# Two of four token tiles get their expert dots from TensorE for all experts, and gather the scores with the values in one row

## The reference, cut to what matters

```python
def peer(h, w_q, keys, u_tab, v_tab):        # u_tab, v_tab: 16384 experts x 1024
    tok = h.reshape(-1, 128, 1024)           # four tiles of 128 tokens
    def block(xb):
        q = (xb @ w_q).reshape(T, 8, 2, 128)
        s = jnp.einsum('thpd,hpnd->thpn', q, keys)
        sv, si = lax.top_k(s, 16)
        cand = sv[:, :, 0, :, None] + sv[:, :, 1, None, :]      # 16 x 16 per head
        cv, ci = lax.top_k(cand.reshape(T, 8, 256), 16)
        eid = i1 * 128 + i2                                     # 8 x 16 = 128 experts per token
        g = jax.nn.softmax(cv, axis=-1)
        u = jnp.take(u_tab, eid, axis=0)
        act = jax.nn.gelu(jnp.einsum('thkd,td->thk', u, xb))
        return jnp.einsum('thk,thkd->td', g * act, jnp.take(v_tab, eid, axis=0))
```

## Time and profile before

| | us |
|---|---|
| median of three runs | 2097.53 (2096.0 to 2109.05) |
| profiled execution: its span, from the first to the last instruction | 2089.7 |
| time around the span, if the profiled execution was as long as the median | 7.8 |
| first gather issued | 582.8 |
| last gather issued | 2067.2 |

### The profile page before, as it was taken

The page is one execution under the profiler, slowest core; times in us unless marked ns, Lnnn a source line. Parts: engine busy times, 40 slices in busy tenths (PEclk is TensorE's granted clock), DMA queues, the critical chain, the costliest instruction groups (busy, mean ns, idle before and its releaser), DMA issues.

```text
span 2089.7 us, 15934 instructions
## 1 busy us (share of the span) xinstructions
PE 1518.5 (73%) x4648; PEld 876.7 (42%) x4648; DVE 1491.0 (71%) x2906; ACT 497.1 (24%) x1412; POOL 878.6 (42%) x658
## 2 busy tenths in 40 slices
PE   7899999889667778887865778655555555556564
PEld 3465787668545555564531445311111111111111
DVE  2545368763276667878598856688898898898876
ACT  2201120111222233223233322222222223222222
POOL 2478404220033333343345434345554555455553
PEclk9899899999879899999987899877777767676677
DMA  8233221124278999999999999799999999999997
GB/s 348 101 139 138 89 79 61 62 77 144 81 308 353 362 351 345 410 392 387 421 393 361 386 378 347 282 413 387 413 412 422 403 409 387 409 417 409 406 418 294
DMA packets 90604, 647.28 MB, mean 310 GB/s; under 512 B 10413, under 2 KB 10773, under 8 KB 12565
## 3 DMA queue, kind: packets, MB, share of 16 engines
q0 software_dynamic: 76448, 555.78, 66.7%
q1 hardware_dynamic: 13376, 90.25, 11.2%
q10 hardware_dynamic: 693, 0.23, 0.0%
HBM read 644.12 MB, written 2.10 MB: 309 GB/s over the span
## 4 chain that ended last, share of the span: by engine, by line
PE 42%; DMA 21%; DVE 19%; issue 8%; ACT 7%; POOL 2%; SPq 0%; DVEq 0%; ACTq 0%; POOLq 0%
DMA arena<-in_peer_uv,arena 21%; PE bank L917 13%; PE bank L671 11%; DVE arena L1642 6%; PE bank L887 6%; PE bank L856 4%; DVE arena L1657 3%; PE bank L707 3%; POOL arena L613 2%; ACT smalls L1138 2%; ACT arena L1133 1%; ACT arena L1128 1%; PE bank L906 1%; PE bank L697 1%; PE bank L800 1%
## 5 line engine op out<-in xcount | busy, mean ns | idle before, releaser
L613 POOL DMA_INDIRECT arena<-in_peer_uv,arena x512 | 688.8, 1345 | 901.4 <-DVE arena L1657 571.1
L917 PE MATMUL bank<-arena,smalls 128*128 128x512 f32 x1024 | 700.9, 822 | 477.6 <-ACT smalls L1138 470.7
L1642 DVE CUSTOM_DVE_ANT_0 arena<-arena 128x1024 f32<-128x1024 f32 x512 | 615.1, 1221 | 87.5 <-DMA arena<-in_peer_uv,arena 86.1
L917 PEld LDWEIGHTS bank<-arena,smalls 128*128 128x128 f32 x1024 | 225.7, 241 | 887.8 <-ACT smalls L1138 675.2
L1657 DVE SCALAR_TENSOR_TENSOR arena<-arena 128x1024 f32<-128x1024 f32 x252 | 322.0, 1278 | 204.8 <-ACT arena L1133 204.8
L671 PE MATMUL bank<-arena 128*128 128x256 f32 (+1 forms) x1216 | 336.1, 433 | 3.6 <-ACT arena L962 3.4
L671 PEld LDWEIGHTS bank<-arena 128*128 128x128 f32 x1216 | 235.9, 195 | 104.6 <-issue 76.0
L1128 ACT ACTIVATE arena<-arena 128x2 f32<-128x2 f32 x256 | 51.9, 203 | 778.0 <-DVE arena L1642 776.3
L887 PE MATMUL bank<-arena 128*128 128x256 f32 x512 | 125.4, 402 | 0.7 <-issue 0.7
L1133 ACT ACTIVATE arena<-arena 128x1 f32<-128x1 f32 x512 | 122.9, 287 | 8.5
L887 PEld LDWEIGHTS bank<-arena 128*128 128x128 f32 x512 | 106.2, 208 | 35.9 <-issue 21.5
(11 more groups left out here) (241 smaller groups left out, 1311.5 us busy)
## 6 DMA issues: line engine op xcount, KB each, us to landing
arena<-in_w_in SPq DMA_DIRECT2D x40, 1024.0 KB, 6.2
arena<-in_w_ada POOLq DMA_DIRECT2D x16, 1024.0 KB, 5.1
arena<-in_w_out SPq DMA_DIRECT2D x16, 1024.0 KB, 6.8
arena<-in_peer_w_q SPq DMA_DIRECT2D x16, 1024.0 KB, 9.9
arena<-in_w_ada SPq DMA_DIRECT2D x8, 1024.0 KB, 9.2
arena<-in_peer_uv,arena POOLq DMA_INDIRECT x512
arena<-in_x SPq DMA_DIRECT2D x4, 512.0 KB, 11.3
out<-arena SPq DMA_DIRECT2D x4, 512.0 KB
```

The lines of the kernel that those rows point to most:

```text
L613: nc.gpsimd.indirect_dma_start(gslot[n % NGS], None, uv_tab[0], bass.IndirectOffsetOnAxis(eid[t % 2][:, k:k + 1], 0)).then_inc(s_gsl[n % N ...
L917: last = mm(acc[h][:, :], diag[:, j % NDG], row_v(n)[:, h * 512:(h + 1) * 512], start=(i == 0), stop=(i == BT - 1))
L1642: V.tensor_tensor_reduce(row_u(n), row_u(n), h2[t], 1.0, 0.0, ALU.mult, ALU.add, dots[:, k:k + 1]).then_inc(s_dot, 1)
```

## The change

Tiles 0 and 1 are gathered as before, but TensorE takes only every fourth row (n % 4 == 3) and VectorE three of four. For tiles 2 and 3:

- a table `vs` in DRAM has one row per expert of 1024 + 256 elements, 5 KB. Its first 4 KB are a copy of the expert's v, made by 64 transfers of 1 MB from DRAM to DRAM on SP's queue between the weight loads of the first part;
- the other 256 elements are gelu of the dot of the expert's u with each of the 256 tokens of tiles 2 and 3. TensorE forms them from a transposed table `u_cols` in 64 chunks of 256 experts (1 MB of load each, 16 products of 128x128 by 128x256), ScalarE drains each chunk with gelu into one of two staging buffers `sst`, SP stores it, with pieces of 1 KB;
- the gather takes the whole 5 KB row. Every token p thus gets 128 scores of each tile's tokens, of which one is its own: a product with the identity (and the gate) on VectorE picks it, as a sum for the even row, as the diagonal matrix itself for the odd row;
- `side` is packed anew: the 80 steps of queries and late mixer stand two to a pair (pairs 0 to 39), then the chunks with 7.0 / 6.5 pairs each and the eight query units of tiles 2 and 3 in two blocks (from pairs 70 and 100). The last chunk stands at pair 121. Pairs 53, 67, 79, 93, 97, 98, 99, 111 and 122 to 127 have no step;
- ahead of the first gather of tile 2 GpSimd waits for all copies and all stores.

```diff
+    NROW = NPK // LT * NA
+    VSW = D + 2 * P
...
+    first = [s for u in units[2:NUA] for s in unit_steps(u)] + late
+    first += [[("h2T", NA)], [("h2T", NA + 1)]]
+    side = [[] for _ in range(NBT)]
+    for n, items in enumerate(first):
+        side[n // 2] += items
+    S_A, S_B = 28, 48
...
+    pace = lambda items: 7.0 if items[0][0] == "S" else 3.0
+    at_j = len(first) / 2
+    for earliest, part in ((0, score(0, S_A)), (0, block[0]), (0, score(S_A, S_B)), (100, block[1]),
+                           (0, score(S_B, NS))):
+        at_j = max(at_j, earliest)
+        for items in part:
+            side[int(at_j)] += items
+            at_j += pace(items) / 6.5
...
+        def by_pe(n):
+            return n % 2 == 1 if n >= NROW else n % 4 == 3
...
+        for n in range(xbc_0, proj_load["gc", 0, 0] + 3 * NX // 2):
+            more = 4 if n < z_0[0] else 2
+            copies[n] = range(copied, min(copied + more, NCOPY))
...
+            def store_scores(c):
+                await_read(sp, ("S", c))
+                dst = vs[c * WCOL:(c + 1) * WCOL, D:VSW].rearrange("(j e) t -> e j t", e=P)
+                sp.dma_start(dst, sst[:, c % 2].rearrange("p j m t -> p j (m t)")).then_inc(s_sst[c % 2], 16)
...
                 sp.dma_start(wring[:, n % WRING].rearrange("p k n -> p (k n)"), w[j]).then_inc(s_w[n % WRING], 16)
+                for i in copies.get(n, ()):
+                    rows_ = slice(i * CROW, (i + 1) * CROW)
+                    sp.dma_start(vs[rows_, VCOL:VCOL + D], uv_tab[0][rows_, D:2 * D]).then_inc(s_vcopy, 16)
+                while stored < NS and s_load[stored] < n - WRING:
+                    store_scores(stored)
+                    stored += 1
+            for c in range(stored, NS):
+                store_scores(c)
...
+                if n == NROW:
+                    pool.wait_ge(s_vcopy, 16 * NCOPY)
+                    for i in range(2):
+                        pool.wait_ge(s_sst[i], 8 * NS)
...
+                    nc.gpsimd.indirect_dma_start(gslot[n % NGS][:, 0:VSW], None, vs, which
+                                                 ).then_inc(s_gsl[n % NGS], 16)
...
+            def expert_scores(c):
+                ps = claim(("S", c))
...
+                w = weights(s_load[c])
+                for j in range(2):
+                    dst = ps[:, j * NA * P:(j + 1) * NA * P].rearrange("p (m t) -> p m t", m=NA)
+                    for k in range(KD):
+                        last = mm(dst, w[:, k, j * P:(j + 1) * P], h2T[:, :, k, :], start=(k == 0), stop=(k == KD - 1))
+                filled(last, ("S", c))
...
+            def expert_scores(c):
+                ps = await_bank(act, ("S", c))
+                if c >= 2:
+                    act.wait_ge(s_sst[c % 2], 16 * (c // 2))
+                release(A(sst[:, c % 2].rearrange("p j m t -> p (j m t)"), ps[:, :], ACT.Gelu_apprx_tanh), ("S", c))
...
+            def pick_dense(j):
...
+                n, k = 2 * j, 2 * j % NE
+                landed(dve, n)
+                V.scalar_tensor_tensor(out=row_s(n), in0=row_s(n), scalar=gate[t % 2][:, k:k + 1], in1=ident[:],
+                                       op0=ALU.mult, op1=ALU.mult, accum_out=dots[:, k:k + 1]).then_inc(s_wd, 1)
+                q = pe_rows[n + 1] - 1
+                landed(dve, n + 1)
+                dve.wait_ge(s_peused, q - NDG + 1)
+                V.scalar_tensor_tensor(out=diag[:, q % NDG], in0=row_s(n + 1), scalar=gate[t % 2][:, k + 1:k + 2],
+                                       in1=ident[:], op0=ALU.mult, op1=ALU.mult).then_inc(s_diagd, 1)
+                rank_on(j)
+                dve.wait_ge(s_wd, j - NROW // 2 + 1)
+                add_value(n, dots[:, k:k + 1])
```

More of the change, by code:

```diff
@@ L8 @@
+import itertools
 from contextlib import ExitStack
@@ L138, in build @@
     NPK = LT * NE
+    NROW = NPK // LT * NA
+    NEXP = u_cols.shape[0] * WCOL
+    NS = u_cols.shape[0]
+    VSW = D + 2 * P
+    VCOL, VLO, SLO = 0, (0, 0), (D, D + P)
     NBT = NPK // 2
@@ L190, in build @@
         add(n + 2 * i + 1, (kind, NA + 1))
[L192 to L199, removed]
+    first = [s for u in units[2:NUA] for s in unit_steps(u)] + late
[4 more added lines that the diff above has]
+    S_A, S_B = 28, 48
+    half_u = (len(units) - NUA) // 2
+    block = [[s for u in units[NUA + i * half_u:NUA + (i + 1) * half_u] for s in unit_steps(u)] for i in range(2)]
+    score = lambda a, b: [[("S", c)] for c in range(a, b)]
+    pace = lambda items: 7.0 if items[0][0] == "S" else 3.0
[6 more added lines that the diff above has]
+            at_j += pace(items) / 6.5
+    assert at_j < NA * BT
     BSEQ = [("h2T", 0)] + sum(unit_steps(units[0]), []) + [("rank", 0), ("norm", 0), ("rank", 1), ("norm", 1)]
@@ L385, in build @@
         s_vcp = sem("products_copied")
+        s_vcopy = sem("values_copied")
+        s_sst = [sem(f"scores{i}_stored") for i in range(2)]
+        s_wd, s_diagd = sem("dense_weight_ready"), sem("dense_diagonal_ready")
         s_fss, s_froot, s_fin, s_out = sem("out_squares"), sem("out_root"), sem("out_ready"), sem("out_stored")
@@ L908, in scores @@
                 filled(last, ("s", m, q4))
-            def add_row(j):
[L912 to L921, removed]
-                    last.then_inc(s_peused, 1)
-                else:
-                    filled(last, ("vs", t, 1))
-                    await_filled(pe, ("vs", t, 1))
-                    nc.tensor.sem_inc(s_peused, 1)
+            def expert_scores(c):
+                ps = claim(("S", c))
+                if c == 0:
+                    await_read(pe, ("h2T", LT - 1, 1))
+                w = weights(s_load[c])
[4 more added lines that the diff above has]
+                filled(last, ("S", c))
@@ new lines, in add_row @@
+            def add_row(j):
+                for n in (2 * j, 2 * j + 1):
+                    if not by_pe(n):
+                        continue
+                    t, q = n // NE, pe_rows[n] - 1
+                    begin = q == (pe_rows[t * NE - 1] if t else 0)
+                    end = pe_rows[n] == pe_rows[(t + 1) * NE - 1]
+                    acc = [claim(("vs", t, h)) if begin else bank_of(("vs", t, h)) for h in range(2)]
+                    if n < NROW:
+                        pe.wait_ge(s_diag, q + 1)
+                    else:
+                        pe.wait_ge(s_diagd, q + 1 - pe_rows[NROW - 1])
+                    landed(pe, n)
+                    for h in range(2):
+                        last = mm(acc[h][:, :], diag[:, q % NDG], row_v(n)[:, h * 512:(h + 1) * 512],
+                                  start=begin, stop=end)
+                        if end and h == 0:
+                            filled(last, ("vs", t, 0))
+                    if end:
+                        filled(last, ("vs", t, 1))
+                        await_filled(pe, ("vs", t, 1))
+                        nc.tensor.sem_inc(s_peused, 1)
+                    else:
+                        last.then_inc(s_peused, 1)
@@ L1633, in _, with rank_on @@
             ranking = None
[L1635 removed]
+            def rank_on(j):
                 nonlocal ranking
[L1638 to L1643 removed]
                 g = j // BP + 2
```

121 lines of the change are left out of this document (80 added, 41 removed).

## The result

| | before | after |
|---|---|---|
| median, us | 2096.77 (2092.9 to 2109.05, 4 runs) | 2274.38 (2269.08 to 2280.21, 4 runs) |
| ratio, 95% interval | | 1.0838 [1.0799, 1.0876] |
| first gather | 582.8 | 588.1 |
| first gather of tile 2 | 1407.96 | 1774.48 |
| last gather | 2067.2 | 2260.4 |

The kernel is 8.4% slower. The forecast was 2231, the result lies 43 us above it, inside the range. Tiles 2 and 3 did get cheaper, 668 to 490 us; tiles 0 and 1 went from 825 to 1186.

A forecast was written before the change was run, and what follows sets the result against it. Tiles 2 and 3 were taken as bound by bytes, tiles 0 and 1 by bytes and hand-written order. Tiles 0 and 1 +351, tiles 2 and 3 -220, copies +3: +134, time 2231 us, range 2060 to 2310.

The forecast's parts named there:

- part 3: Pairs 0 to 39, late mixer at double pace: 345 us, 9.0 a doubled pair; lower end 310, upper 400.
- part 4: The 64 score chunks in tiles 0 and 1: two chunks take L + 10.4, 20.5 us; 64 take 656.
- part 2: Tiles 2 and 3, gathering 5 KB rows: 3.5 us a pair, 448 us against 668, saving 220.
- Part 1: Value copies during the first mixer part, covered by it: +3 us, bounds 0 and +40.
- 6 light ones at 6.45: The six of pairs 0 to 39 outside the 34 doubled ones, taken at 6.45 us each.
- L: Chunk pairs, time for load and store to land: taken as 10.1 us, from 10.0 to 14.4, or 6.
- Part 5: Rest of tiles 0 and 1: query units 111 us, 14 stepless pairs 64; barrier before tile 2 costs nothing.
- Rival (a): Chunk stores land in time, L below 6.9: chunks take 575 us, total 2150; chance 0.22.
- Rival (b): Bytes alone set both stages: tiles 0 and 1 961 us, tiles 2 and 3 412, total 1980; chance 0.20.
- turning point: In Rival (b), the sign turns to faster once tiles 0 and 1 take under 1042 us.
- Rival (c): GpSimd gather issues take 1.68 us through tiles 2 and 3: 507 us, total 2290; chance 0.10.
- Rival (d): Tiles 2 and 3: a 5 KB row takes as long as 8 KB, 220 not saved, 2451 us; chance 0.03.

The follow-up runs named there:

- e1: The changed kernel with four staging buffers for the scores instead of two: 2196.7 us, 1.0482 of before.
- e6: The changed kernel with four staging buffers and ScalarE draining a chunk behind the next pair's weight and diagonal: 2120.2 us, 1.0104 of before.
- a1: The changed kernel with TensorE taking every second row instead of every fourth in pairs 0 to 39: 2321.5 us.
- e3: The changed kernel, two buffers kept, with ScalarE issuing each score store on its own queue right behind its drain: 2233.7 us, 1.0651 of before.
- b1: e6 with nine slots of 5 KB for tiles 2 and 3, the whole computation: 2069.1 us, 0.9861 of before.
- c1 to c4: The changed kernel with rows of 4, 4.5 or 6 KB, then nine 5 KB slots for tiles 2 and 3: 2238.5, 2258.6, 2312.8, 2212.9 us.
- e2: The changed kernel without score stores and their waits, with copies writing the whole 5 KB row: 2199.1 us, 1.0487 of before.

## Why the prediction was right, and where it was off

**Direction and mechanism: right.** Tiles 0 and 1 cost +361 (forecast +351), tiles 2 and 3 saved 178 (forecast 220). The sizes were off by +35 (part 3), -25 (part 4) and +42 (part 2); that the sum is off by only 43 us is in part luck. Where the 361 come from, by the runs: 78 are the wait for the stores (e1), with the slower clock around it; 77 the drain ahead of the next weight (e6); the remaining 206 stay in e6, whose chunk part is at its bytes. 67 MB of loads and 16.8 MB of stores at 407 GB/s are 206 us as well; but since pairs 0 to 39 don't run at that rate, the agreement is only in size.

**Part 1, copies: right.** 3 us forecast; the first gathers lie at 583.3 to 588.9 over the runs with the copies in place, so 0.5 to 6 us. A kernel without copies was not run.

**Part 2, 3.5 us a pair: mis-sized, 3.83 measured.** The prices of the step held: the product takes 0.36 us (0.359 on the page), VectorE 2.7 a pair (347.8 us), the gather's issue 0.95 beside the add; TensorE, with 300.6 us for 128 rows, is below the 3.1 a row of before. What failed is the sentence that I stay close to the byte end because the engines beside it have room. The timeline of one pair after:

```profile
1853.75 0.95 POOL L689 DMA_INDIRECT arena<-values_scores,arena  x1 [1.89 <-DVE arena L1754]
1855.00 0.95 POOL L689 DMA_INDIRECT arena<-values_scores,arena  x1 [0.30 <-issue]
...
1852.21 1.27 DVE L1754 SCALAR_TENSOR_TENSOR arena<-arena 128x1024 f32<-128x1024 f32 x1
...
1854.92 0.40 DVE L1786 SCALAR_TENSOR_TENSOR smalls<-arena,ident 128x128 f32<-128x128 f32 x1 [1.18 <-DMA arena<-values_scores,arena]
```

GpSimd waits for a slot (the add), VectorE waits for a landing. In the chain of waits from 1820 to 1850 a landing takes 7 to 7.6 us. Six slots of 5 KB hold 3.9 MB, and a slot's round is three pairs, 11.5 us: 3.93 / 11.5 is 342 GB/s, the 347 of the window. Before, six slots held 6.3 MB and that was enough for 406. I had named the three pairs of slots and given them no price; nine slots show it, 486 - 410 = 76 us.

**Part 3, 9.0 and 6.45 us a pair: mis-sized, both of them.** 380 against 345. Pairs 0 to 33 end with the second step behind the row of pair 33 (909.96), at 918.8; the windows on both sides of it:

```profile
588.10:918.80 330.70, 272.96 (x1125) 213.46 (x1126) 214.34 (x436) 83.21 (x223) 103.95 (x76) 0.92 0.87 332
918.80:968.10 49.30, 17.21 (x45) 8.83 (x44) 42.23 (x77) 17.60 (x39) 13.63 (x11) 0.62 0.76 287
```

The 34 doubled pairs took 331 us, 9.7 each against 9.0: 25 of the 35 us, though by the chain I had named (a1). The row was priced too low. The 20 rows of this stretch are busy for 58.4 us, 2.9 each and not 1.98, for rows behind idle time ran at the lower clock level; that is 19 us, 13 of them in the doubled pairs. Before, too, a row of tiles 0 and 1 took 2.4 us on the average (305.9 us for all 128). What I had not listed either stands in the chain of waits from 700 to 800:

```profile
711.18 1.28 ACT L1216
712.72 1.28 ACT L1224
714.25 0.31 ACT arena L1229
714.58 1.30 DVE arena L1754
715.97 1.28 DVE arena L1754
...
725.92 14.48 PE bank L746 x64
```

Two activation table loads of ScalarE (1.28 us each) and two adds of VectorE come between some of TensorE's steps. The other 10 us are the "6 light ones at 6.45", taken from the pace of before: pairs 34 to 39 took 49 us instead of 39. VectorE is busy for 42 of them and TensorE for 17: the late normalisation stands two steps to a pair as well, and in the chain of waits it is followed by dots and adds, with ScalarE's squares and table loads between. The upper end, 400, held.

**Part 4, L + 10.4 with L = 10.1: the wait was right and so was its average price, but not what it is made of.** The drain that waits is the one I named: the store of chunk c goes out once chunk c + 1 is filled, and the drain of chunk c + 2 waits for it. But L is not one number. By the packets a store ends 2.0 to 15.4 us behind its issue: for instance 5.4 for the one issued at 1092.10, and 15.4 for the next, issued 6.9 us later. I had both ends in the prediction (6 if the stalled gathers leave the queue free, 14.4 with the dearest store) and took 10.1 between them, for another reason. Nor is there a wait in every two chunks: 23 of 64 drains have one, and TensorE often does both chunks behind a row before it needs the drain. From drain to drain the three runs of chunks took 294.6, 199.9 and 153.7 us, together 648 us for 61 chunks with five bare pairs among them; these taken at the forecast's 3.5, two chunks took 20.7 us, against 20.5. That this fits so closely is luck. The units and the other nine bare pairs came out cheaper: the 158 us outside the three runs of chunks hold three chunks (31 us) and leave 127 against 111 + 46. So the sum is 806 against 831. One slip in the working: L = 8.5 gives 2180 us as the lower end of the forecast's own range, not 2170.

The Trainium skill ("DMA: Bandwidth & Descriptors", Anatomy of one DMA) would have made about 5 us of load and store together, an estimate by its formula for one DMA, which that section gives for DMAs issued by GpSimd (these go out on SP's queue). The trace does not agree: beside a stream of gathers the store behind its load ended after 8.1 us in the median and after up to 15.4, and the store in its own queue took 8.2 (e3).

**Part 5: right.** The barrier costs nothing in after; GpSimd's wait ahead of the first gather of tile 2 is 3.0 us, for VectorE's add, as at any pair.

**Rival (a), 2150: tested as e1, 2197.** The wait goes as described and the chunks follow TensorE's chain. The 47 us above it are the same two terms: pairs 0 to 39 +35 and tiles 2 and 3, partly made up in the units. **Rival (b), 1980:** its floor is real, 650 us for the chunk stretch and 410 for the later stage, but pairs 0 to 39 stay at TensorE's chain, 380 against 310. Its turning point also held in kind: e6 has tiles 0 and 1 at 1033 us, just under the 1042 named, and is still 1% slower since tiles 2 and 3 had not reached 412; with them there, b1 is faster. **Rival (c)** falls. GpSimd's gathers of tiles 2 and 3 have a median of 947 ns beside VectorE's two-input add and the new products; those of tiles 0 and 1, which lie beside the dots, 1686. The rule in the Trainium skill ("GPSIMD Engine Reference", table of specifications), that VectorE's instructions with two SBUF inputs contend with GpSimd, is not borne out by these rows for the add (1.28 us, 128x1024). The dot has two such inputs too, so their number alone does not tell the two apart. **Rival (d)** falls by after itself, 490 us against 668, and by c1 to c4.

## What to carry to other kernels

A staging buffer must outlast the time from its filling to the landing of its store, counted from the place where an in-order queue really issues it; that landing is to be read beside the traffic it will have, not alone. On an in-order engine a drain whose result nobody needs soon belongs behind the next pair's weight, not ahead of it. And a transfer made smaller needs more slots to keep the same bytes in flight: without them a part of its gain stays away, here 76 of 254 us.

## What the runs showed of the hardware that I had not expected

- A 256 KB store with 1 KB pieces, issued behind a 1 MB load in SP's queue and beside the gathers, ended after 2.0 to 15.4 us, median 8.1; from ScalarE's queue the median is 8.2. Its traffic cost nothing that could be measured while TensorE's chain set the pace (e1 against e2).
- TensorE's row of 1.98 us took 3.78 behind an idle time of 7.66 us, at the lower clock level. Over the chunk stretch the 44 rows were busy for 121, 102 and 85 us in after, e1 and e6, at granted clocks of 0.90, 0.96 and 0.97.
- Gathers of 5 KB a partition ran at 405 GB/s with nine slots and 347 with six; those of 6 KB at 390 with six, those of 8 KB at 406. Up to some 405 GB/s the bytes in flight set the rate, not the packet.
- Halving TensorE's work in the chunks and leaving it whole but moving ScalarE's drain gave the same 650 us, both at 0.99 of the DMA engines' time: once the order on ScalarE is right, bytes set the pace and TensorE's 222 us of products cost nothing more.

Open: what the copies cost by themselves, and how the 10 us in the late pairs divide between VectorE's normalisation and what it waits for.
